# GpSimd sums a norm's eight tiles of squares, and TensorE sums the one tile that results

## The chip, the cores and the metric

The kernel runs on one core of one Trainium2 chip. The metric is the device time of one execution in microseconds (us). Three runs of the kernel before took 2425.22, 2431.37 and 2433.13 us; the median is 2431.37.

## The reference, cut to what matters

The reference is one inference step of a two-layer decoder trunk, for 512 prompt tokens and 8 x 8 sample tokens, T = 576 tokens of D = 1024 features in float32. Each layer has two layer norms, so there are four in the program:

```python
def layernorm(x, g, b):
    xf = x.astype(jnp.float32)
    mu = jnp.mean(xf, axis=-1, keepdims=True)
    xc = xf - mu
    var = jnp.mean(xc * xc, axis=-1, keepdims=True)
    return (xc * lax.rsqrt(var + LN_EPS) * g + b).astype(x.dtype)

for l in range(DEPTH):
    x = layernorm(ALPHA * x + token_mixer(x), ln1_g[l], ln1_b[l])
    x = layernorm(ALPHA * x + conv_ffn(x),    ln2_g[l], ln2_b[l])
```

The change touches only `var`, the mean over 1024 features of the centred value squared.

## The kernel before, in words

The activations lie in SBUF with the features on the partitions: `X` is [128, 8, 576], eight tiles of 128 features by 576 tokens. A mean over features is thus a sum over partitions and over the eight tiles. TensorE makes it with a 128x128 matrix of ones as the stationary operand (`C["ones"]`, a part of the constants `CST`): the result stands in every partition of a PSUM bank pair, and each half of 288 tokens has a bank of its own.

The program is written by hand, one instruction stream per engine, ordered by semaphores. A norm `n` (0 to 3; `2 * l` after the mixer, `2 * l + 1` after the FFN) has these steps:

- VectorE has already added the eight tiles of `X` into one tile `XS` while the projection before the norm was running (L1461, L1527). After a drain it raises `n_xs`.
- TensorE sums `XS` over the features (`sum_over_features`, L718) into banks 4 and 5 and raises `n_sum`.
- VectorE centres the eight tiles in place, one instruction each (L1083), and raises `n_xc` after each one.
- ScalarE squares each centred tile into `LSQ` (L404) and raises `n_sq` after each one. Then it loads the activation table for the square root, ahead of its need.
- TensorE multiplies each tile of squares by the ones as it comes, two halves of 288 columns each, and accumulates all eight in banks 6 and 7 (L729). After the last it raises `n_ss`.
- VectorE scales the sum and adds the epsilon into `RN` (L1087), ScalarE takes the square root (L406), VectorE the reciprocal (L1090), then VectorE multiplies each tile by `RN` (L1094), ScalarE applies gain and bias (L409) and rounds into `XH` (L382), and VectorE makes the remainder `XL` (L1068, `n_lo`). The first tile of the next projection on TensorE (L698) takes the eight pieces of `XH` and `XL` as they come. Norm 3 has no projection behind it; there the tiles of `X` are stored.

A float32 matmul on TensorE shows in the trace as two MATMUL records of 128x288, so the 16 matmuls of L729 in a norm are 32 records, and the two of `sum_over_features(4, [XS])` are 4.

GpSimd's stream holds the gathers of the paged cache: per layer it waits for `yc`, starts 64 indirect DMAs (L369) under credits, waits until they have landed, and goes to the next layer. It does no arithmetic. The gathers of a layer are over before the mixer ends, and those of the next layer begin behind that layer's projection. SyncE's queue brings the weights, two buffers deep, and waits for `w_lo` of VectorE; none of its transfers starts between the sum of `XS` and the first rounded tile of a norm.

`XS` and `RN` lie in the first two token tiles of a region that is otherwise the scratch of the mixer and the attention.

Of the kernel before, what the change touches and what calls it, by code (L numbers as in the profile page):

```python
# [5 lines left out]
F32 = mybir.dt.float32  # L6
F32R = mybir.dt.float32r
I32 = mybir.dt.int32
ALU = mybir.AluOpType
# [3 lines left out]
P = 128  # L13
D = 1024
DT = D // P
# [3 lines left out]
T = SEQ + NS  # L19
HT = T // 2  # L20
# [53 lines left out]
def build(nc, x_t, cache_rows, page_table, branch_in, w_uk, w_ukt, w_uv, state_ffn_t, params,  # L74
# [3 lines left out]
    with ctx:  # L78

        TB = T * 4  # L80
# [12 lines left out]
        r_q = region(18432)  # L93
# [7 lines left out]
        def at(name, shape, dt, offset):  # L101
            return nc.alloc_sbuf_tensor_at("m_" + name, shape, dt, offset=base + offset, align_bytes=4)
# [4 lines left out]
        LSQ = at("LSQ", [P, DT, T], F32, r_xs + DT * TB)  # L107
# [85 lines left out]

        XS = at("XS", [P, T], F32, r_q)
        RN = at("RN", [P, T], F32, r_q + TB)

        SFT = at("SFT", [P, 2 * FT, 16], F32, r_z + 22528)
        o = r_z
# [23 lines left out]
        col, C = 0, {}  # L222
# [5 lines left out]
        PS = ctx.enter_context(nc.psum_tensor("PS", [P, 8, 512], F32))  # L228
# [10 lines left out]
        S = {}  # L239
        for names in (  # L240

                "w_landed0 w_landed1 w_hi w_lo",

                "mm_done0 mm_done1 mm_free0 mm_free1",

                "met_pe met_act met_dve past",

                "consts params table x_in0 x_in1 x_in2 x_in3 x_hi y_stored "
                "stored",

                "n_xs n_sum n_xc n_sq n_ss n_var n_std n_xn n_x n_hi n_lo",

                "par_set br_in z_ev v_sum v_centred v_sq v_ss v_var v_std v_scaled v_norm v_turned vt",

                "q_sq q_ss q_var q_std kv_sq kv_ss kv_var kv_std q_lat kv_lat",

                "mask dd ya_mm ya tl sp_mm yc_bias yc",

                "wuk_in wuv_in cq_hi cq_lo ck_hi kr_rot rot_read kpe qn_hi qr rq_mm rq_ev qpe vn_mm "
                "qs_mm qsp_mm",  # L260

                "g_landed0 g_landed1 g_landed2 g_landed3",

                "in_mm in_max in_exp in_turned in_pt in_pv in_set even_mm kt_mm kt_act kt_dve s_mm s_max s_exp p_turned "
                "pt_ev pv_mm o_acc cmb sw_mm cdf cex dg ol_mm ols",

                "wuk2_in pre_hi pre_lo kn_mm kn_hi kn_lo v_mm v_ev",

                "a_s_mm a_max a_exp a_turned a_pt0 a_pt1 a_pv a_yb yt_mm yb_hi yb_lo",

                "xr_hi xr_lo y_hi y_lo m_sum m_hi m_lo",

                "sf_in e_prefix0 e_prefix1 e_free0 e_free1 c_ready silu h_ready h_hi h_lo",
        ):
            for name in names.split():
                S[name] = ctx.enter_context(nc.semaphore("s_" + name))

        def past(e):


            e.sem_inc(S["past"], 1)
# [67 lines left out]
        @block.gpsimd  # L349
        def _(pool):  # L350
            for name, n in CREDIT.items():
                pool.sem_inc(S[name], n)

            for l in range(DEPTH):
                pool.wait_ge(S["yc"], l + 1)
                past(pool)

                for u in range(NU2):
                    b, j = u // 4, u % 4
                    if u == 1:  # L360
                        for other in ("met_pe", "met_act", "met_dve"):
                            pool.wait_ge(S[other], l * N_MEET + 1)
                    if 2 <= u < RAWS:
                        pool.wait_ge(S["s_mm"], l * NU2 + u - 1)
                    pool.wait_ge(S["pv_mm"], CREDIT["pv_mm"] + l * NU2 + u - RAWS + 1)
                    past(pool)
                    for half in range(2):
                        g = b * NG + half * 4 + j
                        pool.indirect_dma_start(  # L369
                            RAW[u % RAWS][:, half, :], None,  # L370
                            cache_rows.rearrange("l n c -> (l n) c"),
                            bass.IndirectOffsetOnAxis(ap=IDXS[:, l, g:g + 1], axis=0))\
                            .then_inc(S[f"g_landed{u % RAWS}"], 16)
                for n in range(RAWS):
                    pool.wait_ge(S[f"g_landed{n}"], 32 * landings(l, n, NU2))
                past(pool)


        @block.scalar
        def _(act):  # L380
# [19 lines left out]
            def norm(n, g0, b0):  # L400
# [4 lines left out]
                act.wait_ge(S["n_var"], n + 1)  # L405
                nc.scalar.activation(RN[:, :], RN[:, :], ACT.Sqrt).then_inc(S["n_std"], 1)  # L406
                for k in range(DT):
# [274 lines left out]
        def _(pe):  # L682
# [31 lines left out]
            def sum_over_features(bank, tiles):  # L714

                for h in range(2):
                    for k, x in enumerate(tiles):
                        mm = pe.matmul(PS[:, bank + h, 0:HT], C["ones"], x[:, h * HT:(h + 1) * HT],  # L718
                                       start=(k == 0), stop=(k == len(tiles) - 1))
                return mm  # L720

            def norm(n):

                pe.wait_ge(S["n_xs"], n + 1)
                sum_over_features(4, [XS]).then_inc(S["n_sum"], 1)
                for k in range(DT):
                    pe.wait_ge(S["n_sq"], n * DT + k + 1)
                    for h in range(2):
                        mm = pe.matmul(PS[:, 6 + h, 0:HT], C["ones"], LSQ[:, k, h * HT:(h + 1) * HT],  # L729
                                       start=(k == 0), stop=(k == DT - 1))  # L730
                mm.then_inc(S["n_ss"], 1)

            ident = C["ident"]
            for l in range(DEPTH):

                for m in range(12):
# [13 lines left out]
                    if m == 7:  # L750
# [6 lines left out]
                        for i in range(2):  # L757
                            mm = pe.transpose(PS[0:NS, 6, i * P:(i + 1) * P], Z[:, 8 + i, SEQ:T], ident)
                        mm.then_inc(S["v_turned"], 1)
                    if m == 8:  # L760
                        pe.wait_ge(S["vt"], l + 1)
                        pe.wait_ge(S["mask"], l + 1)
                        for i in range(2):
# [5 lines left out]
                            for e in range(2):  # L769
                                half = slice(64 * e, 64 * e + 64)  # L770
                                mm = pe.matmul(PS[half, 6, i * NS:(i + 1) * NS],
                                               VT[0:NS, 4, i * P + 64 * e:i * P + 64 * e + 64],
                                               BDW[:, 2 * i + e, :], start=True, stop=True)
# [5 lines left out]
                    if m == 10:  # L779
                        pe.wait_ge(S["z_ev"], l * 10 + 8)  # L780
                        for h in range(2):
                            mm = pe.matmul(PS[:, 4 + h, 0:HT], C["rot"], Z[:, 5, h * HT:(h + 1) * HT],
                                           start=True, stop=True)
# [3 lines left out]
                        for h in range(2):  # L787
                            mm = pe.matmul(PS[:, 6 + h, 0:HT], PWB[:, 0, :], DD[:, 0, h * HT:(h + 1) * HT],
                                           start=True, stop=True)
# [22 lines left out]
                for h in range(2):  # L812
                    mm = pe.matmul(PS[:, 4 + h, 0:HT], PWB[:, 1, :], DD[:, 1, h * HT:(h + 1) * HT], start=True, stop=True)
# [8 lines left out]
                for i in range(4):  # L822
                    for ct in range(KT):
                        for e in range(2):
                            half = slice(64 * e, 64 * e + 64)
                            at0 = (ct * 4 + i) * NS
                            mm = pe.matmul(PS[:, 4 + e, at0:at0 + NS], WUKT[half, i, ct * P:(ct + 1) * P], QS[half, i, :],
                                           start=True, stop=True)
# [3 lines left out]
                for ct in range(KT):  # L832
                    mm = pe.transpose(PS[0:NS, 1, ct * P:(ct + 1) * P], Z[:, 3 + ct, SEQ:T], ident)
                mm.then_inc(S["vn_mm"], 1)
                for u in range(2):
                    pe.wait_ge(S["qpe"], l * 2 + u + 1)
                    for r in range(4):
                        h = 4 * u + r
                        mm = pe.matmul(PS[:, 0, h * NS:(h + 1) * NS], C["sel"][:, r * P:(r + 1) * P], QPE[:, u, SEQ:T],
                                       start=True, stop=True)  # L840
# [4 lines left out]
                for t in range(4):  # L845
# [3 lines left out]
                    mm = pe.matmul(out, QSP[0:ROPE, q], KPF[0:ROPE, SEQ:T], start=False, stop=True)  # L849
# [59 lines left out]
                for t in range(4):  # L909
                    mm = pe.transpose(PS[0:NS, 6, t * P:(t + 1) * P], PRB[:, t * NS:(t + 1) * NS], ident)  # L910
# [4 lines left out]
                for t in range(4):  # L915
                    mm = pe.matmul(PS[:, 7 - t // 2, t % 2 * KL:(t % 2 + 1) * KL], PT[0:NS, t, :], VN[:, :], start=True, stop=True)
# [20 lines left out]
                for ct in range(KT):  # L937
                    for b in range(DB):
                        mm = pe.matmul(PS[:, 4 + ct, b * NS:(b + 1) * NS], OAC[:, b, ct * P:(ct + 1) * P], DG[:, b, :],  # L939
                                       start=True, stop=True)  # L940
# [5 lines left out]
                for i in range(4):  # L946
                    for ct in range(KT):
                        c = slice(i * P, (i + 1) * P)
                        mm = three(PS[:, i, :], WUKH[:, ct, c], WUKL[:, ct, c],
                                   CKH[:, ct, 0:SEQ], CKL[:, ct, 0:SEQ], ct == 0, ct == KT - 1)  # L950
                    mm.then_inc(S["kn_mm"], 1)
                pe.wait_ge(S["pre_lo"], 2 * l + 2)
                for kt in range(4):
                    for ct in range(KT):
                        c = slice(kt * P, (kt + 1) * P)
                        mm = three(PS[:, 4 + kt, :], CKH[:, ct, c], CKL[:, ct, c],
                                   WUVH[:, ct, :], WUVL[:, ct, :], ct == 0, ct == KT - 1)
                    mm.then_inc(S["v_mm"], 1)
                pe.wait_ge(S["v_ev"], l * 5 + 1)
                for h in range(HEADS):  # L960
                    c = slice(h * NS, (h + 1) * NS)
                    for ct in range(KT):
                        mm = pe.matmul(PS[0:NS, 4, c], OLS[:, ct, c], WUV[:, ct, c], start=(ct == 0), stop=(ct == KT - 1))
# [58 lines left out]
                for i in range(4):  # L1022
                    if i >= 2:
                        pe.wait_ge(S["yb_lo"], l * 4 + i - 1)
                    for tt in range(5):
                        n = P if tt < 4 else NS
                        mm = pe.transpose(wide(i % 2)[:, tt * P:tt * P + n], YBT[0:n, tt, i * P:(i + 1) * P],
                                          ident[0:n, 0:n])
# [657 lines left out]
```

## Time and profile before

| | |
|---|---|
| median of three runs | 2431.37 us |
| profiled execution, its own time | 2434.02 us |
| its span | 2432.2 us |
| mean granted TensorE clock, share of full speed | 0.963 |
| PE busy | 2296.1 us, 94% |
| DVE busy | 1188.9 us, 49% |
| ACT busy | 825.8 us, 34% |
| POOL busy | 120.1 us, 5% |

PE is TensorE's matmul stream, PEld its weight loads, DVE is VectorE, ACT is ScalarE and POOL is GpSimd. A busy share is a mean over stages with different limits. PE is busy nearly all the time, but in and around a norm the engines work one after another, so the chain of waits, and not the busy share, says what each piece of a norm costs. Spans of POOL are rough.

### The profile page before, as it was taken

The numbers are of one execution on the slowest core, as the hardware profiler recorded it, in microseconds if no ns is written. First come the engines' busy times: TensorE is split into PE (matmuls) and PEld (weight loads), VectorE is DVE, ScalarE is ACT, GpSimd is POOL, SyncE is SP. The second block draws the span as 40 slices with busy tenths as digits, with TensorE's granted clock in tenths as the row PEclk, the third lists the DMA queues.
The fourth block names the chain that finished last, engine by engine and source line by source line (L and its number), as shares of the span: only waits on it lengthen the run. The fifth ranks groups of instructions, "written<-read, shape, count | busy, mean of one in ns | idle before, by whom it ended". The sixth has DMA issues, their size and how long they took to land.

```text
span 2432.2 us, 43416 instructions
## 1 busy us (share of the span) xinstructions
PE 2296.1 (94%) x17556; PEld 2084.0 (86%) x17556; DVE 1188.9 (49%) x1902; ACT 825.8 (34%) x1478; POOL 120.1 (5%) x132
## 2 busy tenths in 40 slices
PE   8989998999997999999889899989999979999996
PEld 7966666799996999999788666667999969999996
DVE  3744443534346664565347444434333466636654
ACT  3333343423314341332243343334233153313322
POOL 0012220000000000000000122200000000000000
PEclk9989998899998999999999899989999989999998
DMA  5245540022221222222123455400222212322231
GB/s 181 85 137 173 176 157 1 1 87 78 86 83 36 78 92 84 70 85 97 53 83 97 135 176 173 140 1 10 86 85 79 81 38 78 101 75 78 78 102 44
DMA packets 57104, 217.48 MB, mean 89 GB/s; under 512 B 7280, under 2 KB 8176, under 8 KB 56880
## 3 DMA queue, kind: packets, MB, share of 16 engines
q1 hardware_dynamic: 34128, 132.29, 17.1%
q0 software_dynamic: 18432, 75.51, 9.5%
q10 hardware_dynamic: 4448, 8.33, 1.0%
q8 instruction: 70, 1.15, 0.2%
q14 instruction: 26, 0.21, 0.0%
HBM read 211.19 MB, written 4.90 MB: 89 GB/s over the span
## 4 chain that ended last, share of the span: by engine, by line
PE 91%; DVE 4%; ACT 3%; DMA 1%; DVEq 1%; issue 1%; ACTq 0%; SPq 0%
PE PS L698 61%; PE PS L856 5%; PE PS L880 5%; PE PS L900 4%; PE PS L869 2%; PE PS L729 2%; PE PS L1009 1%; PE PS L886 1%; PE PS L718 1%; PE PS L987 1%; ACT m_X L409 1%; PE PS L998 1%; ACT m_XH L382 1%; DVE m_RN L1090 1%; PE PS L939 1%; PE PS L984 1%
## 5 line engine op out<-in xcount | busy, mean ns | idle before, releaser
L698 PE MATMUL PS<-m_XH,m_WH 128*128 128x288 f32 x2560 | 730.0, 299 | 50.8 <-DVE m_XL L1068 38.0
L698 PE MATMUL PS<-m_XL,m_WH 128*128 128x288 f32 x2560 | 721.9, 297 | 0.0
L698 PE MATMUL PS<-m_XH,m_WL 128*128 128x288 f32 x2560 | 553.5, 298 | 0.0
L698 PEld LDWEIGHTS PS<-m_XH,m_WH 128*128 128x128 f32 x2560 | 486.1, 190 | 57.5 <-issue 34.3
L698 PEld LDWEIGHTS PS<-m_XL,m_WH 128*128 128x128 f32 x2560 | 487.2, 190 | 0.5
L698 PEld LDWEIGHTS PS<-m_XH,m_WL 128*128 128x128 f32 x2560 | 414.2, 190 | 0.0
L1068 DVE TENSOR_TENSOR m_WL<-m_WS,m_WH 128x1024 fp32r<-128x1024 f32 (+2 forms) x228 | 292.1, 1281 | 224.1 <-ACT m_WH L382 213.2
L382 ACT ACTIVATE m_WH<-m_WS 128x1024 fp32r<-128x1024 f32 (+2 forms) x228 | 251.8, 1104 | 410.3 <-PE PS L698 403.1
L698 PE MATMUL PS<-m_HH,m_WH 128*128 128x288 f32 x704 | 198.9, 296 | 0.0
L698 PE MATMUL PS<-m_HL,m_WH 128*128 128x288 f32 x704 | 197.6, 295 | 0.0
L369 POOL DMA_INDIRECT m_RAW<-in_cache_rows,m_IDXS x128 | 119.9, 937 | 1443.3 <-DVE m_YC L1265 977.0
L698 PE MATMUL PS<-m_HH,m_WL 128*128 128x288 f32 x704 | 151.6, 297 | 0.0
L856 PE MATMUL PS<-m_CST,m_RAW 128*128 128x128 f32 x1024 | 143.4, 284 | 0.0
L856 PEld LDWEIGHTS PS<-m_CST,m_RAW 128*128 128x128 f32 x1024 | 112.5, 143 | 35.3 <-issue 34.3
L698 PEld LDWEIGHTS PS<-m_HL,m_WH 128*128 128x128 f32 x704 | 132.8, 189 | 0.0
L698 PEld LDWEIGHTS PS<-m_HH,m_WH 128*128 128x128 f32 x704 | 132.5, 188 | 0.0
L880 PE MATMUL PS<-m_KT,m_QSF 128*64 128x256 f32 x1024 | 126.1, 389 | 2.0 <-ACT m_KT L382 2.0
L1480 DVE TENSOR_SCALAR m_CC<-m_EB,m_PAR 128x592 f32<-128x592 f32 x88 | 51.8, 589 | 147.0 <-ACT m_EB L382 147.0
L900 PE MATMUL PS<-m_RAW,m_PT 128*64 128x256 f32 x1024 | 121.5, 379 | 1.4 <-ACT m_PT L382 1.4
L1306 DVE COPY m_KT<-PS 128x512 f32<-128x512 f32 x128 | 88.3, 691 | 66.9 <-PE PS L856 66.5
L1311 DVE TENSOR_SCALAR_CACHE_REDUCE PS<-PS,m_NMX 128x512 f32<-128x512 f32 x64 | 48.6, 759 | 133.0 <-PE PS L880 133.0
L698 PEld LDWEIGHTS PS<-m_HH,m_WL 128*128 128x128 f32 x704 | 112.9, 188 | 0.0
(266 smaller groups left out, 3030.5 us busy)
## 6 DMA issues: line engine op xcount, KB each, us to landing
m_WS<-in_w_units SPq DMA_DIRECT2D x192, 512.0 KB
m_WS<-in_w_units SPq DMA_DIRECT2D x32, 704.0 KB
m_X<-in_x_t SPq DMA_DIRECT2D x4, 576.0 KB, 9.0
m_WS<-in_w_units SPq DMA_DIRECT2D x4, 576.0 KB
out_y<-m_X SPq DMA_DIRECT2D x4, 576.0 KB, 2.8
m_RAW<-in_cache_rows,m_IDXS POOLq DMA_INDIRECT x128, 5.3
m_BRI<-in_branch_in ACTq DMA_DIRECT2D x2, 760.0 KB, 4.9
m_CST<-in_consts SPq DMA_DIRECT2D x1, 1426.5 KB, 13.4
```

The costliest lines, as they stand in the source:

```text
L369: pool.indirect_dma_start(RAW[u % RAWS][:, half, :], None, cache_rows.rearrange("l n c -> (l n) c"), bass.IndirectOffsetOnAxis(ap=IDXS[:, ...
L382: return nc.scalar.activation(out, in_, ACT.Copy)
L698: mm = pe.matmul(PS[0:rows, 2 * par + h, (1 - h) * at0:(1 - h) * at0 + HT], w(part, k), x(k)[:, h * HT:(h + 1) * HT], start=(k == 0 and pa ...
L729: mm = pe.matmul(PS[:, 6 + h, 0:HT], C["ones"], LSQ[:, k, h * HT:(h + 1) * HT], start=(k == 0), stop=(k == DT - 1))
L856: mm = pe.transpose(PS[:, 2 + 2 * half + ct, j * P:(j + 1) * P], RAW[u % RAWS][:, half, c:c + P], ident)
L869: mm = pe.matmul(out[:, :, s % 2, :], QSP[rows, q], RAW[u % RAWS][rows, half, 4 * KL:ROW].rearrange("p (j m) -> p j m", j=4), start=(s % 2 ...
L880: mm = pe.matmul(PS[64 * half:64 * half + 64, k, 0:256], QSF[:, ct, q], keys[:, :, 2 * k:2 * k + 2, :], start=False, stop=(ct == KT - 1))
L900: mm = pe.matmul(PS[64 * half:64 * half + 64, 7, 0:KL], PT[:, j, 64 * half:64 * half + 64], RAW[u % RAWS][:, half, j * KL:(j + 1) * KL], s ...
L1068: return dve.tensor_tensor(out, x, hi.bitcast(F32), ALU.subtract)
L1306: dve.tensor_copy(KT2[:, half, 1, :], PS[:, 3 + 2 * half, :]).then_inc(S["kt_dve"], 1)
L1311: dve.tensor_scalar(PS[:, 0:2, 0:256], PS[:, 0:2, 0:256], -SCALE, NMX[:, b, j:j + 1], ALU.mult, ALU.min, accum_out=NMX[:, b, j + 1:j + 2]) ...
L1480: dve.tensor_scalar(cc, e[:, 2:CV], tap(2), PAR[:, bass.ds(C_CB + c, 1)], ALU.mult, ALU.add)
```

## The change

GpSimd adds the eight tiles of squares into one tile `SS`, seven additions of [128, 576] float32, each behind the square that it needs and each followed by a drain. It then raises the new semaphore `n_sqs`. TensorE waits for that and sums `SS` alone: two matmuls where it had sixteen. The additions of the norms `2 * l` and `2 * l + 1` stand in GpSimd's stream behind the gathers of layer `l`. `SS` takes a third tile in the scratch region, behind `RN`. The rest of the kernel is as it was.

```diff
         XS = at("XS", [P, T], F32, r_q)
         RN = at("RN", [P, T], F32, r_q + TB)
+        SS = at("SS", [P, T], F32, r_q + 2 * TB)
...
                 for n in range(RAWS):
                     pool.wait_ge(S[f"g_landed{n}"], 32 * landings(l, n, NU2))
                 past(pool)
+                for n in (2 * l, 2 * l + 1):
+                    for k in range(1, DT):
+                        pool.wait_ge(S["n_sq"], n * DT + k + 1)
+                        pool.tensor_tensor(SS[:, :], LSQ[:, 0, :] if k == 1 else SS[:, :], LSQ[:, k, :], ALU.add)
+                        pool.drain()
+                    pool.sem_inc(S["n_sqs"], 1)
...
                 pe.wait_ge(S["n_xs"], n + 1)
                 sum_over_features(4, [XS]).then_inc(S["n_sum"], 1)
-                for k in range(DT):
-                    pe.wait_ge(S["n_sq"], n * DT + k + 1)
-                    for h in range(2):
-                        mm = pe.matmul(PS[:, 6 + h, 0:HT], C["ones"], LSQ[:, k, h * HT:(h + 1) * HT],
-                                       start=(k == 0), stop=(k == DT - 1))
-                mm.then_inc(S["n_ss"], 1)
+                pe.wait_ge(S["n_sqs"], n + 1)
+                sum_over_features(6, [SS]).then_inc(S["n_ss"], 1)
```

## Rows read from the trace of the kernel before

**Rows 1.** The page: busy shares, and the chain that ended last by engine.
```profile
PE 2296.1 (94%) x17556; PEld 2084.0 (86%) x17556; DVE 1188.9 (49%) x1902; ACT 825.8 (34%) x1478; POOL 120.1 (5%) x132
PE 91%; DVE 4%; ACT 3%; DMA 1%; DVEq 1%; issue 1%; ACTq 0%; SPq 0%
```

**Rows 2.** Chain of waits across norm 0: start us, us, what.
```profile
740.30 2.30 PE PS L718 x4
742.61 0.02 issue
742.63 0.77 DVE m_X L1083
743.42 0.69 ACT m_LSQ L404
744.11 0.04 issue
744.15 10.54 PE PS L729 x32
754.72 0.77 DVE m_RN L1087
756.22 3.75 DVE m_RN L1090
759.97 0.03 DVEq L1091
760.00 0.04 issue
760.05 0.77 DVE m_X L1094
773.60 16.53 PE PS L698 x121
```

**Rows 3.** Timeline of norm 0: start us, us, engine, line; idle before in brackets.
```profile
743.42 5.33 ACT L404 ACTIVATE m_LSQ<-m_X 128x576 f32<-128x576 f32 x8 [5.30 <-DVE m_X L1083]
748.77 1.28 ACT L406 ACT_TABLE_LOAD   x1
```

**Rows 4.** Timeline, norms 1, 2 and 3: first square, and the instruction behind L729.
```profile
1200.64 5.27 ACT L404 ACTIVATE m_LSQ<-m_X 128x576 f32<-128x576 f32 x8 [5.42 <-DVE m_X L1083]
1212.03 0.76 DVE L1087 TENSOR_SCALAR m_RN<-PS 128x576 f32<-128x576 f32 x1 [6.82 <-PE PS L729]
1953.18 5.33 ACT L404 ACTIVATE m_LSQ<-m_X 128x576 f32<-128x576 f32 x8 [5.00 <-DVE m_X L1083]
1963.77 0.76 DVE L1087 TENSOR_SCALAR m_RN<-PS 128x576 f32<-128x576 f32 x1 [5.97 <-PE PS L729]
2405.02 5.27 ACT L404 ACTIVATE m_LSQ<-m_X 128x576 f32<-128x576 f32 x8 [20.29 <-DVE m_X L1083]
2416.66 0.76 DVE L1087 TENSOR_SCALAR m_RN<-PS 128x576 f32<-128x576 f32 x1 [7.08 <-PE PS L729]
```

**Rows 5.** Stretches of one to three us: busy by engine, PEclk, DMA.
```profile
750.00:751.00 1.00, 1.00 (x6) 0.79 (x5) 0.00 (x0) 0.05 (x1) 0.00 (x0) 1.00 0.00 0
760.00:763.00 3.00, 0.00 (x0) 0.00 (x0) 2.64 (x4) 2.13 (x3) 0.00 (x0) 0.50 0.00 0
1977.00:1978.00 1.00, 1.00 (x6) 1.00 (x6) 0.95 (x2) 1.00 (x2) 0.00 (x0) 0.50 0.00 0
```

**Rows 6.** Groups by line: DVE and ACT on tiles of 128x576; POOL.
```profile
L1461 DVE TENSOR_TENSOR m_XS<-m_XS,m_X 128x576 f32<-128x576 f32 x16 | 12.1, 758 | 1.5
L404 ACT ACTIVATE m_LSQ<-m_X 128x576 f32<-128x576 f32 x32 | 21.2, 683 | 36.0 <-DVE m_X L1083 36.0
L369 POOL DMA_INDIRECT m_RAW<-in_cache_rows,m_IDXS x128 | 119.9, 937 | 1443.3 <-DVE m_YC L1265 977.0 <-PE PS L900 244.2 <-issue 182.2
```

**Rows 7.** Chain of waits behind norm 2: first multiply, then the next tile's end.
```profile
1969.10 0.77 DVE m_X L1094
1982.65 12.36 PE PS L698 x90
```

More of the change, by code:

```diff
@@ L249, in build @@
                 "stored",
-                "n_xs n_sum n_xc n_sq n_ss n_var n_std n_xn n_x n_hi n_lo",
+                "n_xs n_sum n_xc n_sq n_sqs n_ss n_var n_std n_xn n_x n_hi n_lo",
                 "par_set br_in z_ev v_sum v_centred v_sq v_ss v_var v_std v_scaled v_norm v_turned vt",
```

## The prediction

> **What bounds the kernel now.** I read the page first: the reader is to see that PE is busy for 94% of the span and carries 91% of the chain that ended last [rows 1]. That says little about a norm, so I followed the chain of waits through norm 0 [rows 2]. It is a pure relay: TensorE sums the tile XS (2.30 us), VectorE centres the first tile, ScalarE squares it (0.69 us), TensorE's ones-matmuls over the squares take 10.54 us, VectorE takes over 0.03 us later, and the square root, the reciprocal and the first multiply follow one by one until the next projection. No engine has other work under this relay that it could be doing. So whatever is added between the first square and the scaling L1087 ends up in the time, and whatever is taken out of it comes off.
>
> Who is last inside these 10.54 us? The eight squares run from 743.42 to 748.75 us [rows 3], and L1087 starts at 754.72 us. TensorE is six us behind ScalarE when the squares are done. The stretch rows show why: PE is full at 750 us with the granted clock at 1.00, and it is still working through a queue. The relay leg is bound by TensorE, 32 records of it, not by the squares. The change attacks the right leg. The question is only whether seven additions on GpSimd are shorter than what they replace.
>
> **What the leg costs now.** From the start of the first square to the start of L1087: norm 0 754.72 - 743.42 = 11.30 us [rows 2]; norm 1 1212.03 - 1200.64 = 11.39; norm 2 1963.77 - 1953.18 = 10.59; norm 3 2416.66 - 2405.02 = 11.64 [rows 4]. Sum 44.92, mean 11.23 us.
>
> **What the leg costs after the change, step by step.**
> 1. GpSimd's first addition needs two squares. One takes 0.69 us [rows 2] and they come every 5.33 / 8 = 0.67 us [rows 3]: 1.35 us.
> 2. Hand-over from ScalarE to the next engine: 0.04 us, as the "issue" piece between ScalarE and TensorE [rows 2]. The wait costs nothing else: GpSimd has nothing queued behind it but the next norm's additions and, two norms on, the next layer's gathers, which wait for a later projection anyway. Its gathers of the layer are finished by then.
> 3. Seven additions in a row, G us each with their drain. From the second on they are never waiting for a square, if G is over 0.67 us.
> 4. Hand-over to TensorE, 0.04 us.
> 5. Two matmuls, four records, on SS. The same instructions on XS take 2.30 us in norm 0 [rows 2], at the low clock. TensorE will have been idle for over ten us by then; the row of 760 to 763 us shows the granted clock at 0.50 of full, 1.2 GHz, after an idle time of five and more [rows 5]. So I take the 2.30 us of the low level.
> 6. Hand-over to VectorE, 0.02 us [rows 2].
>
> The sum without the additions is 1.35 + 0.04 + 0.04 + 2.30 + 0.02 = 3.75 us. The leg becomes 3.75 + 7G, against 11.23. It breaks even at G = 7.48 / 7 = 1.07 us.
>
> **The price of G.** The trace of before has no addition on GpSimd, only DMA starts of 0.937 us each [rows 6], which say nothing on arithmetic. The bounds:
> - Below: VectorE's own addition of the same shape, 0.758 us [rows 6], and 0.07 us for the drain and the issue behind it, as after the reciprocal [rows 2]: G = 0.83. Leg 9.56 us, 1.67 less, four norms: -6.7 us.
> - Above: the slowest operation on this shape that the trace has, VectorE's reciprocal, 3.75 us [rows 2]: G = 3.82, leg 30.5 us, +77 us. That one is an operation which costs VectorE five times an addition; I keep it as an outer bound and give it next to no weight. Three passes of 0.683 us would be G = 2.12, leg 18.6 us, +29 us.
> - Between: a one-input pass over 128x576 takes ScalarE 0.683 us [rows 6]. An engine that fetches its two operands one after the other would need two such passes: 1.37 us, and 0.07 us behind it: G = 1.44. My estimate is this one: it lies nearer to VectorE's addition than to the reciprocal, and I see no reason why an engine of general-purpose cores should reach VectorE's pace on two operands.
>
> The Trainium skill, "GPSIMD Engine Reference", sections 3.1 and 4.1, speaks against this change: it sends element-wise additions to VectorE and gives GpSimd 4497 ns for a float32 add of 2048 elements per partition, 1.96 times VectorE, because both operands share one read port. Scaled to 576 that would be 1.26 us, as an estimate from that page; with 0.07 us for the drain the leg would be 13.1 us and the four norms 7.3 us longer. No row here shows it.
>
> With G = 1.44 the leg is 3.75 + 10.08 = 13.83 us, 2.60 us more than now; four norms give +10.4 us.
>
> **What the rest does.** TensorE loses 28 of its 32 records per norm. That frees nothing, since TensorE has nothing else to do there. Two things could change behind the leg:
> - The square root's table load (1.28 us behind the last square [rows 3]) stays hidden, with more cover than before: the wait for L1087 grows.
> - The granted clock. Today the long matmul stretch lifts it to 1.00 [rows 5], then it falls again during the reciprocal, and the next projection starts at 0.50. After the change the stretch never lifts it, and the projection starts at 0.50 too. How long it stays there may differ. Norm 2 shows the price: there the clock was still at 0.50 at 1977 us [rows 5], and from the first multiply to the end of the relay it took 1982.65 - 1969.10 = 13.55 us [rows 7]; in norm 0 it took 773.60 - 760.05 = 13.55 us [rows 2]. The pieces come from ScalarE and VectorE at a pace that TensorE can meet at either level, so I cost it at nothing. Without that cover (a low clock all through the first tile and beyond) it would be a microsecond or two per norm.
>
> VectorE is centring tiles while GpSimd's first additions run. If the two disturbed each other, the centring would be delayed by no more than GpSimd is already behind: GpSimd is the slower of the two from the second addition on. That costs nothing, unless it is GpSimd that waits; this goes into the upper part of G.
>
> **Sum.** The profiled execution has a span of 2432.2 us and a time of its own of 2434.0 us; +10.4 gives 2444.4. The median of the three runs is 2431.4, 2.6 us below that execution, and I predict against it: 2431.4 + 10.4 = 2441.8 us.
>
> **Rivals.**
> - *GpSimd adds nearly at VectorE's pace* (the other side). Place: the seven additions. It decides below G = 1.07 us. At G = 0.83 the time is 2424.7 us, at 0.95 (leg 10.4 us) it is 2428.1. For it: both are engines that work on 128 partitions side by side, and the addition is the simplest operation there is. Against it: nothing in the trace shows GpSimd at arithmetic at all. Even the best case is 6.7 us, which is 0.28%, so the change can hardly be faster by a clear margin. Chance 0.12.
> - *A first use costs extra.* GpSimd comes to the additions from DMA starts or a long idle time, and pays once per norm or per layer before the first addition. The nearest row is ScalarE's table load, 1.28 us [rows 3]: four of these on top of 10.4 make 15.5, 2446.9 us. The Trainium skill, "GPSIMD Engine Reference", section 2.1, names about 6 us for the first call into a freshly loaded kernel library; if it were paid in norms 0 and 2, behind the gathers, the time would be 12 us above my forecast, about 2454, and no row of before can show it. Chance 0.10.
> - *GpSimd needs three passes or is held up by VectorE*: G about 1.8 to 2.1 us, +20 to +29 us, 2452 to 2461 us. Chance 0.10.
> - *The change doesn't matter because the squares are late anyway*: against it stands that they are done six us before the leg ends [rows 2, 3]. Chance 0.02.
> - *My forecast*, G between 1.1 and 1.7 us: chance 0.66. Its own range is 2432 to 2449 us.
>
> **How the numbers follow.** 0.3% of the time is 7.3 us; that is about what a measurement of this kernel can tell from no change. Slower by more than that needs G over 1.33 us: most of my own case (0.46 of 0.66), nearly all of the first use and of the slow addition (0.19), together 0.65. Faster by more than 7.3 us asks for less than VectorE's pace, or for a run below the median by chance: 0.05. Within 0.3%: 0.30. The range for 8 in 10 is 2430 to 2454 us: it holds my case, half of the fast one and most of the first use; the bounds of 2424.7 and of 2461 and above stay outside it.
>
> **What would show it right or wrong.** In the trace after: seven GpSimd additions per norm, back to back from the second, start to start about 1.4 us; TensorE's L718 with four records of SS behind them in 2.3 us at a granted clock of 0.50; L1087 starting some 13.8 us after the first square in all four norms, with little scatter, where it now scatters by 1.05 us with the clock's rise. The time from the first multiply to the end of the relay should stay at 13.55 us, and everything outside the norms should stay as it is. It is wrong in its size if the additions come at another pace, since every 0.1 us of G is 2.8 us of the time; it is wrong in its mechanism if the leg after the change is ended by anything but the last addition and the two matmuls, or if the projection behind the norm starts later by more than the leg has grown.

## The result, and the profile after

| | before | after |
|---|---|---|
| median | 2429.97 us (4 runs, 2425.22 to 2433.13) | 2450.77 us (4 runs, 2448.67 to 2456.09) |
| profiled execution: span | 2432.2 us | 2448.0 us |
| legs of norms 0, 1, 2, 3 | 11.30, 11.39, 10.59, 11.64: sum 44.92 us | 19.74, 14.46, 19.74, 14.46: sum 68.40 us |

The changed kernel is slower: the ratio is 1.0091, with a 95% interval of 1.0073 to 1.0109, or +18 to +26 us. A "leg" here, as in the prediction, is the time from the start of a norm's first square to the start of the VectorE instruction that takes the sum (L1087 before, L1090 after). The four legs grew by 23.5 us together, which the interval holds.

The page of the kernel after, busy shares:

```profile
PE 2257.7 (92%) x17444; PEld 2052.2 (84%) x17444; DVE 1189.7 (49%) x1902; ACT 826.5 (34%) x1478; POOL 160.8 (7%) x160
```

PE lost 112 records and 38.4 us of busy time against [rows 1], and POOL got 28 instructions and 40.7 us. None of what PE lost came off the span.

The timeline of norm 0 after (start us, us, engine, line; idle before in brackets), to be held against [rows 2, 3]:

```profile
739.74 5.33 ACT L411 ACTIVATE m_LSQ<-m_X 128x576 f32<-128x576 f32 x8 [5.31 <-DVE m_X L1086]
741.17 1.40 POOL L381 TENSOR_TENSOR m_SS<-m_LSQ 128x576 f32<-128x576 f32 x1 [390.77 <-ACT m_LSQ L411]
747.97 9.09 POOL L381 TENSOR_TENSOR m_SS<-m_SS,m_LSQ 128x576 f32<-128x576 f32 x6 [5.39 <-issue]
757.15 2.29 PE L725 MATMUL PS<-m_SS,m_CST 128*128 128x288 f32 x4 [18.25 <-POOLq L382]
759.48 0.76 DVE L1090 TENSOR_SCALAR m_RN<-PS 128x576 f32<-128x576 f32 x1 [15.12 <-PE PS L725]
```

and that of norm 1:

```profile
1203.45 5.28 ACT L411 ACTIVATE m_LSQ<-m_X 128x576 f32<-128x576 f32 x8 [5.42 <-DVE m_X L1086]
1204.82 1.41 POOL L381 TENSOR_TENSOR m_SS<-m_LSQ 128x576 f32<-128x576 f32 x1 [447.77 <-ACT m_LSQ L411]
1206.38 9.11 POOL L381 TENSOR_TENSOR m_SS<-m_SS,m_LSQ 128x576 f32<-128x576 f32 x6
1215.59 2.29 PE L725 MATMUL PS<-m_SS,m_CST 128*128 128x288 f32 x4 [13.02 <-POOLq L382]
1217.91 0.76 DVE L1090 TENSOR_SCALAR m_RN<-PS 128x576 f32<-128x576 f32 x1 [9.90 <-PE PS L725]
```

Two things are to be seen. Norm 1 is the leg that was forecast, a little longer: seven additions in a row, then 2.29 us of TensorE. Norm 0 has the same and one thing more: the first addition ends at 742.57 us, and the second starts at 747.97 us. The square that it needs, the third, was done by about 741.8 us (739.74 and three squares at 0.67). The bracket says "issue": nothing that the profile shows was waited for. Norm 2 looks like norm 0, norm 3 like norm 1. The two slow norms are the first ones behind the gathers of a layer.

The group of GpSimd's drains after (ns min/median/max) names the instruction in which the time goes by:

```profile
L382 POOLq DRAIN  x28: 1467/1474/6748, 741.1 to 2428.6; - x28
```

`POOLq` is GpSimd's instruction queue. A drain is counted from just ahead of the addition that it follows, and normally ends with it (median 1.47 us, beside an addition of 1.40); the longest is 5.3 us more.

What lies outside the legs is not flat from one profiled execution to the next. Span less legs is 2387.3 us before and 2379.6 after, and between 2376.8 and 2387.4 in the kernels below, none of which touches anything outside the norms but a few instructions behind the gathers. So I read differences in the legs, and the paired intervals, and don't subtract single spans.

### The profile page after: what moved, and what is told of

It reads as the page before. It is cut to its first block, busy times and chain, and to the rows that moved or that the text cites. A ratio compares the mean times of both kernels' runs of the same rounds, so it can differ in the third digit from the quotient of the medians.

```text
span 2448.0 us, 43250 instructions
## 1 busy us (share of the span) xinstructions
PE 2257.7 (92%) x17444; PEld 2052.2 (84%) x17444; DVE 1189.7 (49%) x1902; ACT 826.5 (34%) x1478; POOL 160.8 (7%) x160
## 3 DMA queue, kind: packets, MB, share of 16 engines
q8 instruction: 69, 1.13, 0.2%
## 4 chain that ended last, share of the span: by engine, by line
issue 69%; PE 25%; POOLq 2%; DVE 2%; ACT 1%; DMA 1%; DVEq 0%; another core or an unknown queue 0%; SPq 0%; POOL 0%; ACTq 0%
PE PS L705 6%; PE PS L859 5%; PE PS L883 4%; PE PS L903 4%; PE PS L872 2%; POOLq L382 2%; PE PS L889 1%; PE PS L725 1%; DMA m_CST<-in_consts 1%; ACT m_X L416 0%; DMA m_RAW<-in_cache_rows,m_IDXS 0%; PE PS L851 0%; DVE m_RN L1093 0%; PE PS L808 0%; DVE m_DD L1159 0%
## 5 line engine op out<-in xcount | busy, mean ns | idle before, releaser
L381 POOL TENSOR_TENSOR m_SS<-m_LSQ 128x576 f32<-128x576 f32 x4 | 5.6, 1409 | 1673.3 <-ACT m_LSQ L411 1673.3
```

## Experiments

In the theories, "the gap" is the 5.4 us between the first and the second addition of norms 0 and 2. Legs are in the order of the norms. Every ratio is against the kernel before, with its 95% interval.

**A tiny addition ahead.** My first theory, and the rival of the prediction: code that must come in at the first use.

```diff
+        DUM = at("DUM", [P, 8], F32, r_d)
...
                 past(pool)
+                pool.tensor_tensor(DUM[:, :], C["cos"][:, 0:8], C["sin"][:, 0:8], ALU.add)
                 for n in (2 * l, 2 * l + 1):
```

> One tiny GpSimd addition (128x8) is put right behind the gathers of each layer, hundreds of us ahead of the norm; the rest is the changed kernel. Theory A (the first addition behind the gathers pays about 5.4 us for code that has to come in, once per layer): the tiny addition pays it under TensorE's work, the gap of 5.4 us between the first and the second addition of norms 0 and 2 goes, their leg from the first square to L1090 falls from 19.74 to 14.46 us as in norms 1 and 3, and the time falls by 2 x 5.3 = 10.6 us against the changed kernel, to some 0.4 to 0.5% over the kernel before. Theory B (the gap belongs to where the first large addition stands: its wait, the idle time before it, or the drain behind a first large one): the gap stays in norms 0 and 2 and the time stays 0.9% over the kernel before.

Legs 19.74, 14.45, 19.73, 14.44 us; ratio 1.0103 (1.0086 to 1.0119). The timeline of GpSimd, behind the gathers and in norm 0:

```profile
353.04 0.20 POOL L380 TENSOR_TENSOR m_DUM<-m_CST 128x8 f32<-128x8 f32 x1 [5.14 <-DMA m_RAW<-in_cache_rows,m_IDXS]
739.68 1.41 POOL L384 TENSOR_TENSOR m_SS<-m_LSQ 128x576 f32<-128x576 f32 x1 [386.44 <-ACT m_LSQ L414]
746.49 9.09 POOL L384 TENSOR_TENSOR m_SS<-m_SS,m_LSQ 128x576 f32<-128x576 f32 x6 [5.39 <-issue]
```

The addition was used 386 us ahead, and the gap stands where it stood, to the hundredth. Theory A falls: it is not the first call of an addition. The drains of this kernel are those of the changed one:

```profile
L385 POOLq DRAIN  x28: 1467/1472/6748, 739.6 to 2429.9; - x28
```

**A memset ahead**, `pool.memset(DUM[:, :], 0.0)` at the same place.

> The same place, but a memset of 128x8 in place of the tiny addition. If the 5.4 us is the cost of going from the gathers to any arithmetic on GpSimd, the gap goes from norms 0 and 2 as with the tiny addition. If it belongs to the addition's own code, the memset does not help and norms 0 and 2 keep legs of 19.7 us. I hold the second for likelier, 60 to 40.

Legs 19.74, 14.45, 19.73, 14.43 us (a single execution, 2447.48 us). The gap stays. This came out as I expected, but the reason that I gave, the addition's own code, falls with the run before, so it says only that a memset does not take the gap in either. What the two have in common is that no drain stands behind them.

**The tiny addition with a drain.**

```diff
+        DUM = at("DUM", [P, 8], F32, r_d)
...
                 past(pool)
+                pool.tensor_tensor(DUM[:, :], C["cos"][:, 0:8], C["sin"][:, 0:8], ALU.add)
+                pool.drain()
                 for n in (2 * l, 2 * l + 1):
```

> The tiny addition behind each layer's gathers, now with a drain behind it as the large ones have. Theory A (code of the addition) has fallen: the tiny addition alone left the gap. Theory C: it is the first DRAIN of GpSimd behind the gathers that takes 5.3 us more than the others (the longest of L382 is 6748 ns, the median 1474). Then the new drain pays it hidden, the legs of norms 0 and 2 fall from 19.74 to 14.46 us, and the time falls by 10.6 us to about 0.45% over the kernel before. Theory D (the instructions behind the first large addition aren't there yet when GpSimd gets to them): the gap stays where it is.

Legs 14.50, 14.45, 14.52, 14.44 us; ratio 1.0043 (1.0026 to 1.0060). The gap has gone from both norms, and the two drains of this kernel, the new line first, show where it went:

```profile
L381 POOLq DRAIN  x2: 5524/5536/5548, 357.3 to 1568.0; - x2
L386 POOLq DRAIN  x28: 1472/1474/1497, 744.0 to 2420.6; - x28
```

The new drains take 5.5 us each (0.2 of it is the tiny addition that they follow), far ahead of the norm and under TensorE's work, and the longest of the others is now 1497 ns.

**Only a drain ahead.**

```diff
                 past(pool)
+                pool.drain()
                 for n in (2 * l, 2 * l + 1):
```

> Only a drain behind each layer's gathers, no tiny addition. Theory C in its narrow form (any drain behind the gathers takes in the 5.3 us): legs of norms 0 and 2 at 14.46 us, as with the tiny addition and its drain. If the drain must follow an addition to take it in, the gap stays here and goes only with the addition ahead of it. Theory D: the gap stays.

```profile
L378 POOLq DRAIN  x2: 5281/5286/5292, 354.9 to 1569.2; - x2
L383 POOLq DRAIN  x28: 1472/1472/1502, 742.3 to 2426.0; - x28
```

Legs 14.51, 14.45, 14.52, 14.46 us. The narrow form of theory C holds: a drain with nothing of GpSimd's arithmetic to drain, behind the gathers, takes 5.29 us, and the drains after it are ordinary. It isn't a wait for something that would end by itself: it costs 5.3 us here, right behind the last landing, and 5.3 us in the kernel with the tiny addition, where the first drain comes 386 us later. This kernel's time can't show the gain: its single execution took 2447.52 us, with 2387.4 us outside the legs, the most of all kernels here. That the time comes down with the gap is shown by the run before, whose interval lies below that of the changed kernel.

**No drain at all.**

```diff
-                        pool.tensor_tensor(SS[:, :], LSQ[:, 0, :] if k == 1 else SS[:, :], LSQ[:, k, :], ALU.add)
-                        pool.drain()
-                    pool.sem_inc(S["n_sqs"], 1)
+                        if k > 1:
+                            pool.wait_ge(S["n_ssk"], n * (DT - 2) + k - 1)
+                        pool.tensor_tensor(SS[:, :], LSQ[:, 0, :] if k == 1 else SS[:, :], LSQ[:, k, :], ALU.add)\
+                            .then_inc(S["n_ssk" if k < DT - 1 else "n_sqs"], 1)
```

> No drain on GpSimd: each addition raises a semaphore when it is complete, and the next one waits for that. Theory C: no drain, no gap; the legs of all four norms are equal. The pitch of the additions, now 1.54 us, of which 1.40 is the addition, changes by what the semaphore costs against the drain, between 0 and -0.1 us: legs of 13.8 to 14.5 us, and the time 0.35 to 0.45% over the kernel before. Theory D: the gap of 5.4 us stays behind the first addition of norms 0 and 2.

Legs 14.47, 14.40, 14.46, 14.40 us. The chain of waits in norm 0:

```profile
739.03 1.42 POOL m_SS L383
740.45 0.02 issue
740.47 0.02 POOLq L382
740.49 0.10 issue
740.59 1.42 POOL m_SS L383
```

The gap is gone without any drain being paid elsewhere, and the pitch of the additions is 740.59 - 739.03 = 1.56 us here, and 1.54 with drains: an ordinary drain costs no more than a semaphore. For the legs the upper part of my expectation held. The time came out higher than the 0.35 to 0.45% that I expected: the ratio was 1.0062 (1.0045 to 1.0078). The legs alone make +12.8 us, 0.53%, which is inside.

**TensorE's work kept.**

It has the tiny addition ahead, as in the first experiment, which takes nothing of the gap away. The edit on TensorE:

```diff
                 sum_over_features(4, [XS]).then_inc(S["n_sum"], 1)
+                for k in range(DT):
+                    pe.wait_ge(S["n_sq"], n * DT + k + 1)
+                    for h in range(2):
+                        mm = pe.matmul(PS[:, 6 + h, 0:HT], C["ones"], LSQ[:, k, h * HT:(h + 1) * HT],
+                                       start=(k == 0), stop=(k == DT - 1))
                 pe.wait_ge(S["n_sqs"], n + 1)
                 sum_over_features(6, [SS]).then_inc(S["n_ss"], 1)
```

> The kernel with the tiny addition ahead, and TensorE also multiplies the eight single tiles of squares as before the change (32 records more per norm); their sum is then overwritten by that of SS, so they are work for nothing. If TensorE's saved work is worth nothing and only its clock matters, the four records of SS run at the high clock where they ran at the low one: 1.2 us in place of 2.3, and the legs fall from 14.46 to about 13.4 us in every norm, 4 us in all. If the saved work is worth something, the legs grow.

Legs 19.75, 13.43, 19.73, 13.41 us; ratio 1.0081 (1.0068 to 1.0095). No drain stands ahead of the norm, so it has the gap. In norms 1 and 3 the leg is 1.03 us shorter than after the change, with 32 records more on TensorE. The timeline of norm 1:

```profile
1206.42 10.42 PE L739 MATMUL PS<-m_LSQ,m_CST 128*128 128x288 f32 x32 [1.63 <-ACT m_LSQ L414]
1217.84 1.24 PE L728 MATMUL PS<-m_SS,m_CST 128*128 128x288 f32 x4 [0.99 <-POOLq L385]
```

The same four records take 1.24 us here, and 2.29 us in the changed kernel. The rows of the granted clock say why, first of this kernel in norm 1, then of the changed kernel in norm 0, where TensorE had been idle for over 18 us (busy by engine, PEclk, DMA):

```profile
1218.00:1219.00 1.00, 1.00 (x4) 0.52 (x4) 0.00 (x0) 0.00 (x0) 0.00 (x0) 1.00 0.00 0
```

```profile
757.00:759.50 2.50, 2.29 (x4) 1.17 (x4) 0.02 (x1) 0.00 (x0) 0.05 (x1) 0.50 0.00 0
```

1.00 is 2.4 GHz and 0.50 is 1.2 GHz. In norms 0 and 2 of this kernel nothing was won, a part that I had wrong: there the gap leaves TensorE idle for 6.17 and 5.98 us before the sum, and the four records took 2.29 us again. So in norms 1 and 3 taking the single tiles off TensorE was worth less than nothing: it costs the level of the clock for the sum that remains.

**VectorE as the adder.**

GpSimd's additions are taken out; on VectorE, behind the centring:

```diff
+                for k in range(1, DT):
+                    dve.wait_ge(S["n_sq"], n * DT + k + 1)
+                    dve.drain()
+                    dve.tensor_tensor(SS[:, :], LSQ[:, 0, :] if k == 1 else SS[:, :], LSQ[:, k, :], ALU.add)
+                dve.drain().then_inc(S["n_sqs"], 1)
                 dve.wait_ge(S["n_ss"], n + 1)
```

> The seven additions go to VectorE, behind its eight centring instructions, and TensorE sums one tile; GpSimd has no arithmetic. The first addition starts when the centring ends, 5.4 us behind its start, seven additions with drains take 7 x 0.83 = 5.8 us, and TensorE 2.3 us at the low clock: a leg of about 4.6 + 5.8 + 2.4 = 12.8 us in each norm, against 11.2 before the change and 14.46 to 19.74 with it: +6 us or 0.26% against the kernel before. If the change lost only because of the engine it chose, this one would be no slower than the kernel before; I expect that taking TensorE off the tiles one by one costs even with the faster adder, since the additions are serial behind the last centred tile.

```profile
747.93 0.76 DVE L1086 TENSOR_TENSOR m_SS<-m_LSQ 128x576 f32<-128x576 f32 x1
748.77 4.93 DVE L1086 TENSOR_TENSOR m_SS<-m_SS,m_LSQ 128x576 f32<-128x576 f32 x6
753.78 2.29 PE L719 MATMUL PS<-m_SS,m_CST 128*128 128x288 f32 x4 [11.38 <-DVEq L1087]
```

Legs 12.87, 12.82, 12.87, 12.81 us; ratio 1.0033 (1.0021 to 1.0044). VectorE adds at a pitch of 0.83 us, little more than half of GpSimd's 1.54, though it starts three us later. It still loses to the kernel before. Against the kernel with the tiny addition and its drain, the same form on GpSimd, the legs are 6.5 us shorter: that is the engine's part. The 6.5 us that they are still longer than before belong to the form (all seven additions in series, and only then TensorE).

**Half of the change, on GpSimd and on VectorE.** TensorE takes tiles 0 to 3 as before; tiles 4 to 7 are added into one, and TensorE sums that last (here GpSimd's version; in VectorE's the same three additions stand behind its centring).

```diff
                 past(pool)
+                pool.drain()
                 for n in (2 * l, 2 * l + 1):
-                    for k in range(1, DT):
+                    for k in range(5, DT):
                         pool.wait_ge(S["n_sq"], n * DT + k + 1)
-                        pool.tensor_tensor(SS[:, :], LSQ[:, 0, :] if k == 1 else SS[:, :], LSQ[:, k, :], ALU.add)
+                        pool.tensor_tensor(SS[:, :], LSQ[:, 4, :] if k == 5 else SS[:, :], LSQ[:, k, :], ALU.add)
...
+                for k in range(4):
+                    pe.wait_ge(S["n_sq"], n * DT + k + 1)
+                    for h in range(2):
+                        pe.matmul(PS[:, 6 + h, 0:HT], C["ones"], LSQ[:, k, h * HT:(h + 1) * HT],
+                                  start=(k == 0), stop=False)
                 pe.wait_ge(S["n_sqs"], n + 1)
-                sum_over_features(6, [SS]).then_inc(S["n_ss"], 1)
+                for h in range(2):
+                    mm = pe.matmul(PS[:, 6 + h, 0:HT], C["ones"], SS[:, h * HT:(h + 1) * HT],
+                                   start=False, stop=True)
+                mm.then_inc(S["n_ss"], 1)
```

> Half of the change: TensorE takes the first four tiles of squares as they come (16 records), GpSimd adds the last four into one (three additions), and TensorE sums that one behind them. A drain right behind the gathers takes the 5.3 us in out of the way. GpSimd can start when square 6 is done, 4.0 us behind the first square's start, and three additions of 1.54 us end at 8.7 us; TensorE is through its 16 records at about 7.4 us, waits, and takes 1.2 us for the last four at the high clock: legs of 9.9 to 10.0 us in place of 11.2, -5 us or -0.2%. If any handing over to GpSimd costs more than it saves, the legs are over 11.2 us.

> The same half, with VectorE as the adder and GpSimd without arithmetic. VectorE has centred its last tile 4.6 us behind the first square's start, three additions with drains take 2.5 us and end at 7.1 us; TensorE ends its 16 records at about 7.4 us and goes on at once with the last four at the high clock: legs of 8.6 us in place of 11.2, -10 us or -0.43% against the kernel before. If it were no better than the half on GpSimd, the adder would not be what decides.

GpSimd's half: legs 9.96, 9.89, 9.95, 9.90 us, sum 39.70; ratio 0.9989 (0.9974 to 1.0003), so the 5 us are there in the legs, and in the time they can't be told from none. VectorE's half: legs 8.54, 8.40, 8.31, 8.25 us, sum 33.50; ratio 0.9969 (0.9957 to 0.9982), faster. The timeline of norm 0 with GpSimd's half, then with VectorE's:

```profile
740.76 6.81 PE L737 MATMUL PS<-m_LSQ,m_CST 128*128 128x288 f32 x16 [1.57 <-ACT m_LSQ L412]
745.66 2.94 POOL L382 TENSOR_TENSOR m_SS<-m_SS,m_LSQ 128x576 f32<-128x576 f32 x2
748.70 1.24 PE L741 MATMUL PS<-m_SS,m_CST 128*128 128x288 f32 x4 [1.13 <-POOLq L383]
```

```profile
742.80 6.80 PE L730 MATMUL PS<-m_LSQ,m_CST 128*128 128x288 f32 x16 [1.56 <-ACT m_LSQ L405]
747.42 1.59 DVE L1093 TENSOR_TENSOR m_SS<-m_SS,m_LSQ 128x576 f32<-128x576 f32 x2
749.44 1.13 PE L734 MATMUL PS<-m_SS,m_CST 128*128 128x288 f32 x4
```

With GpSimd TensorE waits 1.13 us for the last sum; with VectorE it waits for nothing. Both have the sum at the high clock, granted 1.00 in its stretch. This is what the change was after. It works on VectorE, which adds while TensorE multiplies; on GpSimd, even with the drain out of the way, no gain in time is shown.

**Rounded squares.** TensorE's own cost per tile, in place of fewer tiles. This changes the arithmetic: the squares are rounded to the form that the projections' operands have (by how much the outputs move is not shown here). The edit is against the kernel before.

```diff
-        LSQ = at("LSQ", [P, DT, T], F32, r_xs + DT * TB)
+        LSQ = at("LSQ", [P, DT, T], F32R, r_xs + DT * TB)
+        ONR = at("ONR", [P, P], F32R, r_d)
...
+                if n == 0:
+                    act.wait_ge(S["consts"], 16)
+                    copy(ONR[:, :], C["ones"])
...
-                        mm = pe.matmul(PS[:, 6 + h, 0:HT], C["ones"], LSQ[:, k, h * HT:(h + 1) * HT],
+                        mm = pe.matmul(PS[:, 6 + h, 0:HT], ONR[:, :], LSQ[:, k, h * HT:(h + 1) * HT],
```

> The kernel before, but ScalarE writes the squares in the rounded float32 form that the projections' operands have, against a ones matrix in the same form, so that each of the 16 ones-matmuls of a norm is one record and not two, at 0.12 us pitch at the high clock and 0.24 at the low where two records take 0.49 and 0.98. If the leg was bound by TensorE's float32 passes alone, TensorE keeps up with the squares (0.67 us each, 0.48 us of TensorE at the low clock), and the leg is the squares' 5.4 us and the last tile's 0.6: 6.0 us in place of 11.2, -21 us or -0.85%. If the idle TensorE or its clock hurts behind the norm, part of that comes back.

```profile
741.10 5.34 ACT L409 ACTIVATE m_LSQ<-m_X 128x576 fp32r<-128x576 f32 x8 [4.67 <-DVE m_X L1088]
741.83 5.50 PE L734 MATMUL PS<-m_LSQ,m_ONR 128*128 128x288 f32 x16 [1.57 <-ACT m_LSQ L409]
747.37 0.76 DVE L1092 TENSOR_SCALAR m_RN<-PS 128x576 f32<-128x576 f32 x1 [1.66 <-PE PS L734]
```

Legs 6.27, 6.21, 6.26, 6.21 us, sum 24.95; ratio 0.9904 (0.9887 to 0.9920), median 2405.52 us. TensorE ends 0.9 us behind the last square, where it ended 5.9 us behind [rows 2, 3]. And it does so at the low clock: the granted clock is 0.50 from 742 to 747 us. It beats both kernels by more than any rearrangement of additions, and GpSimd has no part in it.

The legs and the intervals side by side (a leg sum as a share of 2430 us):

| kernel | sum of legs, us | against before, us | as a share | measured, 95% |
|---|---|---|---|---|
| after | 68.40 | +23.5 | +0.97% | +0.73 to +1.09% |
| tiny addition | 68.36 | +23.4 | +0.96% | +0.86 to +1.19% |
| TensorE's work kept | 66.32 | +21.4 | +0.88% | +0.68 to +0.95% |
| tiny addition and drain | 57.91 | +13.0 | +0.53% | +0.26 to +0.60% |
| no drain | 57.73 | +12.8 | +0.53% | +0.45 to +0.78% |
| VectorE adds all | 51.37 | +6.5 | +0.27% | +0.21 to +0.44% |
| GpSimd's half | 39.70 | -5.2 | -0.21% | -0.26 to +0.03% |
| VectorE's half | 33.50 | -11.4 | -0.47% | -0.43 to -0.18% |
| rounded squares | 24.95 | -20.0 | -0.82% | -1.13 to -0.80% |

The two kernels of one execution each, with the memset and with the drain alone, have no interval and are left out. The legs, each sum from one profiled execution, lie inside the interval in eight of nine; VectorE's half gave back a little of its legs, and I can't name where.

## Why the prediction was right, and where it was not

The sign held, and so did the mechanism: in all four norms the leg is ended by the last addition and the two matmuls, and the relay behind it did not get longer. The size was half of what came: 2441.8 us forecast, 2450.8 measured. That is inside the range of 2430 to 2454, but outside the 2432 to 2449 that the forecast gave for its own case: without the room left for its rivals it would have missed. The sign that all four legs would be alike, with little scatter, did not come true: two are 5.3 us longer. By its steps:

- **Steps 1 and 2**, the start of the first addition: 741.17 - 739.74 = 1.43 us; forecast 1.39 after the first square's start.
- **Step 3**, the additions. The operation was taken at 1.37 us and takes 1.40. The nearness is in part luck: the 1.37 is two passes of ScalarE, and no run here shows that GpSimd takes its time for the reason given, two operands one after the other. The term that was too small is what stands between two of them: 0.07 us was read from VectorE's drain and its issue, GpSimd needs 0.14. So G was 1.54 in place of 1.44 us: 28 x 0.10 = +2.8 us. The Trainium skill, "GPSIMD Engine Reference", section 3.1, gives 4497 ns for 2048 elements; the 1.26 us scaled from it, an estimate, lies further below the 1.40 measured. Its rule that additions belong on VectorE agrees with the 0.83 and 1.54 us of the two adders here.
- **The step that failed** is the price of the drain in the same term: "0.07 us for the drain and the issue behind it, as after the reciprocal". It was priced by another engine's row, as if it were the same everywhere and each time. The first drain of GpSimd behind the indirect DMAs costs 5.3 us more, twice in the program: +10.6 us. The runs with a drain ahead, and the one without drains, show it.
- **Steps 4 to 6**: four records of SS in 2.29 us at a granted clock of 0.50, in all four norms, as forecast. The prediction held this for a plain price; the run with TensorE's work kept shows in norms 1 and 3 that 1.03 us of it is a loss that the change brings with it.
- **Behind the leg**: norm 0 after still had the clock at 0.50 at 771 us, as [rows 5] had in norm 2, and the relay did not get longer: in norm 1 it goes from 1223.25 us to 1236.82, 13.57 us against the 13.55 of [rows 2, 7]. The zero was right, as far as the rest of the span, which moves by up to ten us from one profile to the next, lets it be seen. The row of the clock in norm 0 after:

```profile
771.00:772.00 1.00, 1.00 (x6) 1.00 (x5) 0.95 (x2) 1.00 (x2) 0.00 (x0) 0.50 0.00 0
```

The sum mended by the two terms is 10.4 + 2.8 + 10.6 = 23.8 us; the legs grew by 23.5.

VectorE's centring, which the prediction feared for, was not disturbed: its eight instructions take 5.41 us in norm 1 before and after, and GpSimd's first addition, which runs beside it, takes 1.41 us, against 1.40 of the later ones.

**The rivals.** GpSimd at VectorE's pace is out: 1.40 against 0.76 us. Three passes are out. "A first use costs extra" got a chance of 0.10, and it had the place right (the norms behind the gathers, once per layer) and a price between its two figures (1.28 and about 6 us), but not the cause. The Trainium skill, "GPSIMD Engine Reference", section 2.1, names about 6 us for the first call to a freshly loaded kernel, close to the 5.4 us of the gap; the tiny addition, which moved the first call away and left the gap, shows that it isn't the first call of the addition here. A figure that fits is no proof of its cause. The runs that told them apart were the one that moved the addition and not the drain, and the one that moved the drain alone.

## What to carry to other kernels

Look at how an engine's steps overlap before moving work off it: TensorE was the slow one of this leg, but it worked alongside the squares. A chain of additions that must end before TensorE starts has therefore to beat TensorE's remainder behind the last square (5.9 us here), and not its whole busy time (10.5 us). Handing over all tiles lost with either engine. Handing over the last four while TensorE takes the first won 0.3% with VectorE; with GpSimd it came out even. Where an engine is slow on a small reduction, first ask what form its operands have, and whether the result allows another; and on GpSimd, after indirect DMAs, chain by semaphores, or spend one drain where something hides it.

## What the hardware showed that I had not expected

- The first DRAIN on GpSimd behind a run of indirect DMAs takes 5.29 us alone (5281 to 5292 ns, two with the drain alone and two again with GpSimd's half); the next ones end with the addition before them. It costs the same 386 us after the last landing, and nothing is paid where no drain stands (the chain of semaphores). What it does in this time stays open: no run here looks inside it.
- The kernel after has two MODIFY_POOL_CONFIG records at 355.4 us, behind the first layer's gathers, which the kernel before has not. They are not the cause: the gap shows in the second layer as well, where there is no such record; the kernel without drains has the two records, at 358.1 us, and no gap; and with the drain alone they stand at 360.3 us, behind the 5.3 us.
- A float32 addition of 128x576 on GpSimd takes 1.40 us, and its span varies little (1396 to 1414 ns over 24, where VectorE's of the same shape takes 757 to 760).
- Four ones-matmul records take 1.24 us at the high level of the clock and 2.29 us at the low one (granted 1.00 and 0.50): an engine that is relieved of work can be slower at what it keeps.
